# Expert weights read in runs of 16 KB, two or four adjacent rows a partition

## The chip, the cores and the metric

One core of one Trainium2 chip runs the whole program. The metric is the device time of one execution in microseconds, the median of several runs; lower is better.

## What is computed

One decoder layer on 256 tokens of width 1024, in float32: a recurrent branch and an attention branch are mixed, and then comes a mixture of 32 experts, of which each token takes 4. The experts are what this case is about:

```python
N_EXPERTS = 32; TOP_K = 4; D_MODEL = 1024; D_EXPERT = 1024   # 256 tokens

def expert_block(args):
    xb, e = args
    gu = xb @ w_gu[e] + b_gu[e]                      # w_gu[e]: 1024 x 2048
    x_glu = jnp.minimum(gu[:, :D_EXPERT], SWIGLU_LIMIT)
    x_lin = jnp.clip(gu[:, D_EXPERT:], -SWIGLU_LIMIT, SWIGLU_LIMIT)
    act = x_glu * jax.nn.sigmoid(SWIGLU_ALPHA * x_glu) * (x_lin + 1.0)
    return act @ w_down[e] + b_down[e]               # w_down[e]: 1024 x 1024
```

Every expert's weights are read whole: 8 MB of `w_gu` and 4 MB of `w_down` each, 384 MB in all.

## The kernel before

Each engine has one program, written out by hand, and semaphores join them. SyncE (SP) issues nearly all DMAs, in one queue, in the order of its code; a wait in SP's code holds everything behind it.

First come 20 blocks of 2 MB of the dense matrices (`w_in`, `w_proj_rnn`, `w_proj_attn`, `w_out`), which land in two buffers `land` and are split by ScalarE (`w_hi`) and GpSimd (`w_lo`) for TensorE; SP loads block u when `lo_ready` says that block u - 2 is done with (L260). Between these blocks, SP already loads what it can of experts 0 and 1 into places that earlier tiles have left: parts of gate and up weights ("gu") of expert 1 at u = 11, 12, 14, 15 and 16, parts of the down weights ("dn") of expert 0 at u = 13 and 18, the rest behind the last block (L294 to L312). The semaphore `filled` counts finished halves of the dense products (40 in all), `lg_filled` the router's logits.

Then come the experts. gu has two sets of eight 1 MB buffers (`gu[par][k]`, one for each step k of 128 rows of the contraction), dn one set of four buffers of 1 MB (`dn[j]`, two k-steps each; the last is filled by two DMAs). SP reloads a gu buffer when `gu_used` says that TensorE has finished with it two experts before, a dn buffer when `dn_used` says so one expert before. In the loop up to expert 15 (`TURN` = 8 pairs) the queue holds gu of expert e + 1 ahead of dn of expert e; from then on it is gu(e), dn(e), gu(e + 1).

TensorE's part of an expert (`expert`, L617 to L673): bias rows, 32 gate and up matmuls (L635) with the 64 tokens of the expert (`xg`) as weights, transposes of the gates (L643), the gather of the next expert's tokens (L587), some matmuls that only keep the clock up (L394), four transposes of the activation (L654), 16 down matmuls (L663), and four that add the weighted rows to the sums (L670). A float32 matmul shows as two records. VectorE's part, between the gate matmuls and the transposes: clamp the gate half (L1171) and the up half (L1172) out of PSUM, join them (L1174), multiply by ScalarE's sigmoid (L1178), take the next expert's tokens out of PSUM into `xg` (L1145), and copy the transposed activation (L1182).

Ahead of the experts, L1084 (VectorE, tokens 0 to 127) and L848 (ScalarE, the others) write the normalised tokens `hn`; the first gather (L600) reads them as weights, 128 channels at a time, and L1152 scales them by the norm's vector `V_GFFN`. So the contraction's channels are cut into eight runs of 128 adjacent ones, like the rows of `w_gu`.

Of the kernel before, what the change touches and what calls it, by code (L numbers as in the profile page):

```python
# [52 lines left out]
V_GMIX, V_CONVW, V_CONVB, V_BX, V_BA, V_AP, V_GFFN, N_VEC = 0, 1, 5, 6, 7, 8, 9, 10  # L53


def program(nc, x, vecs, rope, w_in, lru_wx, lru_wa, w_proj_rnn, w_proj_attn, w_out,
# [7 lines left out]
    with ctx:  # L64
# [43 lines left out]
        x1T, hn = at("x1T", 24, [P, KT, T]), at("hn", 168, [P, TT, D])  # L108
# [6 lines left out]
        gu = [[at(f"gu{par}_{k}", 96 * par + 8 * k, [P, 2 * D]) for k in range(KT)] for par in range(2)]  # L115
        dn = [at(f"dn{j}", 64 + 8 * j, [P, 2, D]) for j in range(4)]
# [53 lines left out]

        x_landed = [sem(f"x_landed{t}") for t in range(TT)]
# [4 lines left out]
        gu_landed = [[sem(f"gu_landed{p}_{k}") for k in range(KT)] for p in range(2)]  # L176
        dn_landed = [sem(f"dn_landed{j}") for j in range(5)]
# [56 lines left out]
        def _(sp):  # L234
# [8 lines left out]
            def load_gu(row, par, wait, ks=range(KT)):  # L243
                for k in ks:
                    wait(k)
                    sp.dma_start(gu[par][k][:, :], w_gu_rows[ds(row + k * P, P), :]).then_inc(gu_landed[par][k], 16)  # L246

            def load_dn(row, wait, js=range(4)):
                for j in js:
                    wait(j)  # L250
                    src = w_dn_rows[ds(row + j * 2 * P, 2 * P), :].rearrange("(k p) n -> p k n", p=P)
                    if j < 3:
                        sp.dma_start(dn[j][:, :, :], src).then_inc(dn_landed[j], 16)  # L253
                    else:
                        for c in range(2):
                            sp.dma_start(dn[j][:, c, :], src[:, c, :]).then_inc(dn_landed[j + c], 16)  # L256

            for u, src in enumerate(blocks):
# [35 lines left out]
                if u == 11:  # L294
                    load_gu(D, 1, lambda k: sp.wait_ge(b96_landed, 48), [3])
                if u == 12:
                    load_gu(D, 1, lambda k: sp.wait_ge(hglo_ready, 1), [5])
                if u == 13:
                    load_dn(0, lambda j: sp.wait_ge(hg_ready, 1), [3, 2])
                if u in (14, 15):  # L300
                    load_gu(D, 1, lambda k: sp.wait_ge(s_filled, H), [u - 14])
                if u == 16:
                    load_gu(D, 1, lambda k: sp.wait_ge(filled, 28), [2])
                if u == 18:
                    load_dn(0, lambda j: sp.wait_ge(filled, 32), [1])
            load_dn(0, lambda j: sp.wait_ge(filled, 36), [0])
            load_gu(D, 1, lambda k: sp.wait_ge(filled, 36), [4])
            load_gu(D, 1, lambda k: sp.wait_ge(mix_ready, 4), [6, 7])
            load_gu(0, 0, lambda k: sp.wait_ge(lo_ready, 76 if k < 2 else 80), range(0, 3))
            load_gu(0, 0, lambda k: sp.wait_ge(filled, 39), [4, 6])  # L310
            load_gu(0, 0, lambda k: sp.wait_ge(filled, 40), [5, 7])
            load_gu(0, 0, lambda k: sp.wait_ge(lg_filled, 1), [3])  # L312

            def load_pair(E, row):
                load_gu(row, 0, lambda k: sp.wait_ge(gu_used, KT * E + (k + 1 - 2 * KT)))
                load_dn(row, lambda j: sp.wait_ge(dn_used, 4 * E + (j + 1 - 4)))
                load_gu(row + D, 1, lambda k: sp.wait_ge(gu_used, KT * E + (k + 1 - KT)))
# [70 lines left out]
        def _(pe):  # L388
# [228 lines left out]
            def expert(E, X, par, meanwhile=None, first=False):  # L617
# [622 lines left out]
```

## Time and profile before

| | us |
|---|---|
| median of 3 runs | 1256.97 (1255.77 to 1258.02) |
| span of the profiled execution | 1254.1 |
| TensorE busy | 1174.0 (94%) |
| VectorE, ScalarE, GpSimd busy | 341.2, 219.5, 221.3 |
| DMA queue of SP, share of the 16 engines | 89.5%, 449.07 MB |

The span is that of one profiled execution, from first to last instruction; the profile does not give that execution a time of its own, and the median lies 2.9 us above the span. The page cuts the span into 40 slices and gives for each the busy share of an engine in tenths (9 is 90% or more), the clock that TensorE was granted, and what the DMA engines moved:

```profile
## 2 busy tenths in 40 slices
PE   8969789999999999999999999999999999999996
...
PEclk9989999999999999999999999999999999999998
DMA  9434446679899999999999999999999999999994
GB/s 255 164 134 143 142 165 245 229 260 383 343 417 416 417 418 418 418 418 418 418 418 418 418 413 418 418 418 418 418 418 417 418 418 418 418 418 418 418 417 197
```

A slice is 31.4 us. The first nine or so are the dense part, the rest the experts.

### The profile page before, as it was taken

How to read it: one execution, taken by the hardware profiler on the slowest of the kernel's cores; microseconds unless marked ns; L12 is line 12 of the kernel's file. 1: busy time of each engine (PE TensorE's matmuls, PEld its weight loads, DVE VectorE, ACT ScalarE, POOL GpSimd, SP SyncE). 2: the span in 40 equal slices, each digit the busy share in tenths (PEclk: the TensorE clock that was granted, in tenths of full speed). 3: DMA queues.
4: the chain of work that ended last, by engine and by line, in shares of the span. 5: the costliest groups of instructions: out<-in, count | busy, mean ns of one | idle time of the engine just before them, and what ended most of it. 6: DMA issues, size and time to landing. Idle time of an engine off the chain costs nothing.

```text
span 1254.1 us, 18900 instructions
## 1 busy us (share of the span) xinstructions
PE 1174.0 (94%) x7653; PEld 604.0 (48%) x7653; DVE 341.2 (27%) x595; ACT 219.5 (17%) x361; POOL 221.3 (18%) x99
## 2 busy tenths in 40 slices
PE   8969789999999999999999999999999999999996
PEld 8859789999333333333333333333333333333332
DVE  5972685332311111221111111111211111111112
ACT  5436635545100000000000000000000000000001
POOL 6838966784000000000000000000000000000000
PEclk9989999999999999999999999999999999999998
DMA  9434446679899999999999999999999999999994
GB/s 255 164 134 143 142 165 245 229 260 383 343 417 416 417 418 418 418 418 418 418 418 418 418 413 418 418 418 418 418 418 417 418 418 418 418 418 418 418 417 197
DMA packets 98784, 450.03 MB, mean 359 GB/s; under 512 B 10721, under 2 KB 12833, under 8 KB 65825
## 3 DMA queue, kind: packets, MB, share of 16 engines
q1 hardware_dynamic: 98608, 449.07, 89.5%
q8 instruction: 22, 0.36, 0.1%
q0 software_dynamic: 144, 0.52, 0.1%
q14 instruction: 10, 0.07, 0.0%
HBM read 448.00 MB, written 1.05 MB: 358 GB/s over the span
## 4 chain that ended last, share of the span: by engine, by line
PE 60%; DMA 14%; issue 7%; SPq 7%; POOL 7%; ACT 2%; DVE 2%; POOLq 0%; DVEq 0%
PE ps L635 25%; PE ps L663 13%; DMA gu<-in_w_gu 10%; POOL w_lo L368 6%; DMA dn<-in_w_down 4%; PE ps L670 3%; SPq L246 3%; PE ps L587 3%; PE ps L394 2%; PE ps L421 2%; PE ps L418 2%; PE ps L417 2%; SPq L253 2%; SPq L256 2%; DVE actT L1182 1%
## 5 line engine op out<-in xcount | busy, mean ns | idle before, releaser
L635 PE MATMUL ps<-gu,xg 128*64 128x512 f32 x2048 | 448.9, 593 | 7.2 <-DMA gu<-in_w_gu 7.2
L635 PEld LDWEIGHTS ps<-gu,xg 128*64 128x64 f32 x2048 | 142.0, 137 | 296.0 <-issue 263.8
L663 PE MATMUL ps<-dn,actT 128*64 128x512 f32 x1024 | 228.1, 596 | 10.3 <-DVE actT L1182 6.0
L368 POOL TENSOR_TENSOR w_lo<-land,w_hi 128x1024 fp32r<-128x1024 f32 x80 | 216.1, 2729 | 76.1 <-ACT w_hi L715 76.0
L1171 DVE TENSOR_SCALAR g<-ps 128x512 f32<-128x512 f32 x32 | 22.1, 692 | 746.4 <-PE ps L635 746.4
L663 PEld LDWEIGHTS ps<-dn,actT 128*64 128x64 f32 x1024 | 72.0, 137 | 154.0 <-issue 137.5
L863 ACT ACTIVATE wT<-ps 128x256 f32<-128x256 f32 x32 | 12.3, 384 | 539.3 <-PE ps L643 539.3
L417 PE MATMUL ps<-x_hi,w_hi 128*128 128x256 f32 x384 | 95.8, 287 | 4.1 <-ACTq L753 2.9
L418 PE MATMUL ps<-x_lo,w_hi 128*128 128x256 f32 x384 | 94.9, 284 | 0.0
L715 ACT ACTIVATE w_hi<-land 128x1024 fp32r<-128x1024 f32 x80 | 80.1, 1052 | 55.1 <-PE ps L421 39.4
L670 PE MATMUL ps<-y_sb,wT 64*128 64x512 f32 x256 | 63.6, 615 | 22.2 <-ACT y_sb L869 22.2
L869 ACT ACTIVATE y_sb<-ps 128x512 f32<-128x512 f32 x32 | 19.1, 597 | 329.4 <-PE ps L663 329.4
L417 PEld LDWEIGHTS ps<-x_hi,w_hi 128*128 128x128 f32 x384 | 74.1, 193 | 4.5 <-issue 4.5
L418 PEld LDWEIGHTS ps<-x_lo,w_hi 128*128 128x128 f32 x384 | 74.2, 193 | 0.1
L394 PE MATMUL ps<-ones 128*128 128x512 bf16 x254 | 66.8, 386 | 0.0
L421 PE MATMUL ps<-x_hi,w_lo 128*128 128x256 f32 x384 | 55.2, 287 | 5.2 <-POOL w_lo L368 5.2
L670 PEld LDWEIGHTS ps<-y_sb,wT 64*128 64x128 f32 x256 | 22.0, 186 | 65.4 <-ACT y_sb L869 50.4
L421 PEld LDWEIGHTS ps<-x_hi,w_lo 128*128 128x128 f32 x384 | 50.2, 194 | 6.6 <-POOL w_lo L368 6.4
L587 PE MATMUL ps<-sel,part 128*128 128x64 bf16 x1536 | 50.0, 193 | 0.0
L587 PEld LDWEIGHTS ps<-sel,part 128*128 128x128 bf16 x1536 | 49.2, 98 | 0.4
L394 PEld LDWEIGHTS ps<-ones 128*128 128x128 bf16 x254 | 23.0, 99 | 15.7 <-issue 0.8
L1182 DVE COPY actT<-ps 128x512 f32<-128x512 f32 x32 | 22.1, 692 | 7.7 <-PE ps L654 3.2
(246 smaller groups left out, 929.0 us busy)
## 6 DMA issues: line engine op xcount, KB each, us to landing
gu<-in_w_gu SPq DMA_DIRECT2D x256, 1024.0 KB, 19.3
dn<-in_w_down SPq DMA_DIRECT2D x96, 1024.0 KB, 19.7
dn<-in_w_down SPq DMA_DIRECT2D x64, 512.0 KB, 17.9
land<-in_w_in SPq DMA_DIRECT2D x13, 2048.0 KB, 8.0
land<-in_w_proj_rnn SPq DMA_DIRECT2D x2, 2048.0 KB, 8.9
land<-in_w_proj_attn SPq DMA_DIRECT2D x2, 2048.0 KB, 8.9
land<-in_w_out SPq DMA_DIRECT2D x2, 2048.0 KB, 7.8
land<-in_w_in SPq DMA_DIRECT2D x2, 1024.0 KB, 8.8
```

The lines of the kernel that those rows point to most:

```text
L246: sp.dma_start(gu[par][k][:, :], w_gu_rows[ds(row + k * P, P), :]).then_inc(gu_landed[par][k], 16)
L368: pool.tensor_tensor(w_lo[:, q % PIECES], land[q // PIECES][:, :, (q % PIECES) * P:(q % PIECES + 1) * P], w_hi[:, q % PIECES].bitcast(f32) ...
L394: mm(ps[:, bank, :], ones[:, :], ones[:, :].unsqueeze(1).to_broadcast([P, 4, P]), start=True, stop=True)
L417: mm(to, w_hi[:, b, k, :], src_hi[:, k, :], start=k == 0, stop=False)
L418: mm(to, w_hi[:, b, k, :], src_lo[:, k, :], start=False, stop=False)
L421: last = mm(to, w_lo[:, b, k, :], src_hi[:, k, :], start=False, stop=k == KT - 1)
L587: last = mm(ps[:, 6, k * SLOTS:(k + 1) * SLOTS], part[q][:, t, k * P:(k + 1) * P], sel[buf][:, t, :], start=n == 0, stop=n == 3 * TT - 1)
L635: last = mm(ps[64 * h:64 * h + 64, 4 + c, :], xg[:, k * SLOTS:(k + 1) * SLOTS], gu[par][k][:, c * D + h * HALF:c * D + (h + 1) * HALF], st ...
L663: last = mm(ps[64 * h:64 * h + 64, 6, :], actT[:, k % 4, (k // 4) * SLOTS:(k // 4 + 1) * SLOTS], dn[k // 2][:, k % 2, h * HALF:(h + 1) * H ...
L670: mm(ps[:, 2 * t + h, :], wT[64 * h:64 * h + 64, t * P:(t + 1) * P], y_sb[64 * h:64 * h + 64, :], start=False, stop=False)
L715: A(w_hi[:, q % PIECES], land[u % LAND][:, :, (q % PIECES) * P:(q % PIECES + 1) * P], ACT.Copy).then_inc(hi_ready, 1)
L1182: V.tensor_copy(actT[:, :, :], ps[:, 7, :].rearrange("p (j s) -> p j s", j=4)).then_inc(actT_ready, 1)
```

## The change

- The rows of `w_gu` are cut another way. A buffer is now 2 MB, and partition p gets two adjacent rows of 8 KB, rows 8p + 2m and 8p + 2m + 1 for buffer m, in one run of 16 KB. k-step k then contracts the channels 8p + k. One DMA fills one buffer: four an expert, not eight.
- `w_down` likewise: a buffer holds half of the rows, partition p four adjacent rows of 4 KB (16 KB). Two DMAs of 2 MB an expert, not five.
- The channels of the tokens are reordered to match: L1084 and L848 read `x_sb` with a step of 8 elements and write `hn` contiguously, and the norm's vector is there a second time in that order (`V_GROW`).
- The columns of the activation are reordered to match `w_down`: L1171 and L1172 read PSUM with a step of 4 elements and write contiguously.
- `gu_used`, `dn_used` and the landing semaphores count 4 and 2 an expert. The early loads sit at other places in the queue, and `x1T` moves from 24 KB to 184 KB, so that the last gu buffers of expert 0 no longer wait for the logits.

```diff
-        x1T, hn = at("x1T", 24, [P, KT, T]), at("hn", 168, [P, TT, D])
+        x1T, hn = at("x1T", 184, [P, KT, T]), at("hn", 168, [P, TT, D])
...
-        gu = [[at(f"gu{par}_{k}", 96 * par + 8 * k, [P, 2 * D]) for k in range(KT)] for par in range(2)]
-        dn = [at(f"dn{j}", 64 + 8 * j, [P, 2, D]) for j in range(4)]
+        gu = [[at(f"gu{par}_{m}", 96 * par + 16 * m, [P, GU_RUN, 2 * D]) for m in range(4)] for par in range(2)]
+        dn = [at(f"dn{h}", 64 + 16 * h, [P, DN_RUN, D]) for h in range(2)]
...
+        hn_rows = hn[:, :, :].rearrange("q t (k p) -> q t k p", k=KT)
+        x_rows = x_sb[:, :, :].rearrange("q t (p k) -> q t k p", k=KT)
+
+        def by_rows(t):
+            return t.rearrange("q (j p) -> q j p", j=DN_RUN)
+
+        def by_columns(t):
+            return t.rearrange("q (p j) -> q j p", j=DN_RUN)
...
-            def load_gu(row, par, wait, ks=range(KT)):
-                for k in ks:
-                    wait(k)
-                    sp.dma_start(gu[par][k][:, :], w_gu_rows[ds(row + k * P, P), :]).then_inc(gu_landed[par][k], 16)
-
-            def load_dn(row, wait, js=range(4)):
-                for j in js:
-                    wait(j)
-                    src = w_dn_rows[ds(row + j * 2 * P, 2 * P), :].rearrange("(k p) n -> p k n", p=P)
-                    if j < 3:
-                        sp.dma_start(dn[j][:, :, :], src).then_inc(dn_landed[j], 16)
-                    else:
-                        for c in range(2):
-                            sp.dma_start(dn[j][:, c, :], src[:, c, :]).then_inc(dn_landed[j + c], 16)
+            def load_gu(row, par, wait, ms=range(4)):
+
+                src = w_gu_rows[ds(row, D), :].rearrange("(p k) n -> p k n", p=P)
+                for m in ms:
+                    wait(m)
+                    sp.dma_start(gu[par][m][:, :, :], src[:, GU_RUN * m:GU_RUN * m + GU_RUN, :]).then_inc(
+                        gu_landed[par][m], 16)
+
+            def load_dn(row, wait, hs=range(2)):
+
+                for h in hs:
+                    wait(h)
+                    src = w_dn_rows[ds(row + h * HALF, HALF), :].rearrange("(p j) n -> p j n", p=P)
+                    sp.dma_start(dn[h][:, :, :], src).then_inc(dn_landed[h], 16)
...
-                if u == 11:
-                    load_gu(D, 1, lambda k: sp.wait_ge(b96_landed, 48), [3])
-                if u == 12:
-                    load_gu(D, 1, lambda k: sp.wait_ge(hglo_ready, 1), [5])
                 if u == 13:
-                    load_dn(0, lambda j: sp.wait_ge(hg_ready, 1), [3, 2])
-                if u in (14, 15):
-                    load_gu(D, 1, lambda k: sp.wait_ge(s_filled, H), [u - 14])
+                    load_dn(0, lambda h: sp.wait_ge(hg_ready, 1), [1])
+                if u == 15:
+                    load_gu(D, 1, lambda m: sp.wait_ge(s_filled, H), [0])
                 if u == 16:
-                    load_gu(D, 1, lambda k: sp.wait_ge(filled, 28), [2])
-                if u == 18:
-                    load_dn(0, lambda j: sp.wait_ge(filled, 32), [1])
-            load_dn(0, lambda j: sp.wait_ge(filled, 36), [0])
-            load_gu(D, 1, lambda k: sp.wait_ge(filled, 36), [4])
-            load_gu(D, 1, lambda k: sp.wait_ge(mix_ready, 4), [6, 7])
-            load_gu(0, 0, lambda k: sp.wait_ge(lo_ready, 76 if k < 2 else 80), range(0, 3))
-            load_gu(0, 0, lambda k: sp.wait_ge(filled, 39), [4, 6])
-            load_gu(0, 0, lambda k: sp.wait_ge(filled, 40), [5, 7])
-            load_gu(0, 0, lambda k: sp.wait_ge(lg_filled, 1), [3])
+                    load_gu(D, 1, lambda m: sp.wait_ge(filled, 28), [1])
+            load_dn(0, lambda h: sp.wait_ge(filled, 36), [0])
+            load_gu(D, 1, lambda m: sp.wait_ge(filled, 36), [2])
+            load_gu(D, 1, lambda m: sp.wait_ge(mix_ready, 4), [3])
+            load_gu(0, 0, lambda m: sp.wait_ge(lo_ready, 76 + 4 * m), [0, 1])
+            load_gu(0, 0, lambda m: sp.wait_ge(filled, 40), [2, 3])
...
-                load_gu(i * (2 * D), 0, lambda k: sp.wait_ge(gu_used, KT * (2 * i) + (k + 1 - 2 * KT)))
-                load_dn(i * (2 * D) - D, lambda j: sp.wait_ge(dn_used, 8 * i + (j + 1 - 8)))
-                load_gu(i * (2 * D) + D, 1, lambda k: sp.wait_ge(gu_used, KT * (2 * i) + (k + 1 - KT)))
-                load_dn(i * (2 * D), lambda j: sp.wait_ge(dn_used, 8 * i + (j + 1 - 4)))
-            load_dn((2 * TURN - 1) * D, lambda j: sp.wait_ge(dn_used, 8 * TURN + (j + 1 - 8)))
+                load_gu(i * (2 * D), 0, lambda m: sp.wait_ge(gu_used, 4 * (2 * i) + (m + 1 - 8)))
+                load_dn(i * (2 * D) - D, lambda h: sp.wait_ge(dn_used, 4 * i + (h + 1 - 4)))
+                load_gu(i * (2 * D) + D, 1, lambda m: sp.wait_ge(gu_used, 4 * (2 * i) + (m + 1 - 4)))
+                load_dn(i * (2 * D), lambda h: sp.wait_ge(dn_used, 4 * i + (h + 1 - 2)))
+            load_dn((2 * TURN - 1) * D, lambda h: sp.wait_ge(dn_used, 4 * TURN + (h + 1 - 4)))
...
-                for k in range(KT):
-                    pe.wait_ge(gu_landed[par][k], 8 * E + 16)
-                    if first and k == 4:
+                for m in range(4):
+                    pe.wait_ge(gu_landed[par][m], 8 * E + 16)
+                    if first and m == 2:
                         pe.wait_ge(xg_ready, 1)
-                    for c in range(2):
-                        for h in range(2):
-                            last = mm(ps[64 * h:64 * h + 64, 4 + c, :], xg[:, k * SLOTS:(k + 1) * SLOTS],
-                                      gu[par][k][:, c * D + h * HALF:c * D + (h + 1) * HALF],
-                                      start=False, stop=k == KT - 1)
+                    for r in range(GU_RUN):
+                        k = GU_RUN * m + r
+                        for c in range(2):
+                            for h in range(2):
+                                last = mm(ps[64 * h:64 * h + 64, 4 + c, :], xg[:, k * SLOTS:(k + 1) * SLOTS],
+                                          gu[par][m][:, r, c * D + h * HALF:c * D + (h + 1) * HALF],
+                                          start=False, stop=k == KT - 1)
                     last.then_inc(gu_used, 1)
...
-                for k in range(KT):
-                    if k % 2 == 0 or k == KT - 1:
-                        pe.wait_ge(dn_landed[(k + 1) // 2], 16 * E + 16 * (par + 1))
-                    for h in range(2):
-                        last = mm(ps[64 * h:64 * h + 64, 6, :], actT[:, k % 4, (k // 4) * SLOTS:(k // 4 + 1) * SLOTS],
-                                  dn[k // 2][:, k % 2, h * HALF:(h + 1) * HALF], start=k == 0, stop=k == KT - 1)
-                    if k % 2 == 1:
-                        last.then_inc(dn_used, 1)
+                for half in range(2):
+                    pe.wait_ge(dn_landed[half], 16 * E + 16 * (par + 1))
+                    for j in range(DN_RUN):
+                        for h in range(2):
+                            last = mm(ps[64 * h:64 * h + 64, 6, :], actT[:, j, half * SLOTS:(half + 1) * SLOTS],
+                                      dn[half][:, j, h * HALF:(h + 1) * HALF],
+                                      start=half == 0 and j == 0, stop=half == 1 and j == DN_RUN - 1)
+                    last.then_inc(dn_used, 1)
...
-            A(hn[:, 1, :], x_sb[:, 1, :], ACT.Copy, scale=rstd2[:, 1:2]).then_inc(hn_ready, 1)
+            A(hn_rows[:, 1], x_rows[:, 1], ACT.Copy, scale=rstd2[:, 1:2]).then_inc(hn_ready, 1)
...
-            V.tensor_scalar(hn[:, 0, :], x_sb[:, 0, :], rstd2[:, 0:1], None, ALU.mult).then_inc(hn_ready, 1)
+            V.tensor_scalar(hn_rows[:, 0], x_rows[:, 0], rstd2[:, 0:1], None, ALU.mult).then_inc(hn_ready, 1)
...
-                dve.wait_ge(gu_used, KT * E + KT * (par + 1))
-                V.tensor_scalar(g1[:, :], ps[:, 4, :], LIMIT, None, ALU.min).then_inc(glu_ready, 1)
-                V.tensor_scalar(l1[:, :], ps[:, 5, :], LIMIT, -LIMIT, ALU.min, ALU.max).then_inc(gu_read, 1)
+                dve.wait_ge(gu_used, 4 * E + 4 * (par + 1))
+                V.tensor_scalar(by_rows(g1[:, :]), by_columns(ps[:, 4, :]), LIMIT, None, ALU.min).then_inc(glu_ready, 1)
+                V.tensor_scalar(by_rows(l1[:, :]), by_columns(ps[:, 5, :]), LIMIT, -LIMIT, ALU.min, ALU.max).then_inc(gu_read, 1)
```

## Rows read from the trace of the kernel before

**Rows 1.** Windows: range, us, busy PE, PEld, DVE, ACT, POOL, clock, DMA share, GB/s.

```profile
318.00:1235.00 917.00, 877.56 (x5402) 325.86 (x5400) 158.43 (x354) 52.75 (x99) 0.70 (x1) 1.00 1.02 417
```

**Rows 2.** Chain of waits inside one expert: start us, us, what (x records).

```profile
403.11 13.73 PE ps L635 x64
...
416.84 0.37 PE ps L643 x2
...
418.61 1.08 PE ps L394 x5
...
421.20 7.11 PE ps L663 x32
...
431.52 8.58 PE ps L635 x39
```

**Rows 3.** The first clamp's line: duration ns min/median/max, first and last start.

```profile
L1171 DVE TENSOR_SCALAR g<-ps x32: 691/692/693, 328.9 to 1228.7; 128x512 f32<-128x512 f32 x32
```

**Rows 4.** Chain of waits at other experts, same columns as rows 2.

```profile
315.06 13.73 PE ps L635 x64
...
374.69 13.74 PE ps L635 x64
...
648.54 3.67 PE ps L663 x16
...
749.08 13.74 PE ps L635 x64
...
976.40 13.73 PE ps L635 x64
```

**Rows 5.** Waits: engine, line, releaser: us in total, times, longest.

```profile
PEld ps L635 <- DMA gu<-in_w_gu: 26.5, 27, 1.5
...
PEld ps L663 <- DMA dn<-in_w_down: 15.1, 18, 1.5
```

**Rows 6.** Packets and bytes of the whole span, from the page.

```profile
DMA packets 98784, 450.03 MB, mean 359 GB/s; under 512 B 10721, under 2 KB 12833, under 8 KB 65825
```

**Rows 7.** Windows, columns as rows 1; in the first two only gu moves, then only dn.

```profile
354.00:370.00 16.00, 15.39 (x120) 6.30 (x118) 4.90 (x11) 1.38 (x3) 0.00 (x0) 1.00 1.01 421
...
1147.00:1163.00 16.00, 15.31 (x74) 4.86 (x70) 0.00 (x0) 0.60 (x1) 0.00 (x0) 1.00 1.01 420
...
374.00:380.00 6.00, 6.00 (x32) 2.09 (x32) 0.00 (x0) 0.00 (x0) 0.00 (x0) 1.00 1.03 412
...
494.00:500.00 6.00, 6.00 (x30) 1.97 (x28) 0.00 (x0) 0.00 (x0) 0.00 (x0) 1.00 1.02 408
```

**Rows 8.** Windows around the first expert, columns as rows 1.

```profile
278.00:296.00 18.00, 17.98 (x148) 17.59 (x147) 3.45 (x5) 8.83 (x13) 15.01 (x7) 1.00 1.00 407
296.00:300.00 4.00, 4.00 (x36) 4.00 (x35) 0.69 (x1) 2.67 (x10) 1.78 (x7) 1.00 0.56 193
...
313.00:319.00 6.00, 6.00 (x38) 3.05 (x39) 5.15 (x8) 2.76 (x3) 0.00 (x0) 1.00 0.23 66
```

**Rows 9.** VectorE ahead of the experts: two lines, and where L1089 starts (start us, us).

```profile
L1084 DVE TENSOR_SCALAR hn<-x_sb,stat x1: 754/754/754, 306.4 to 306.4; 128x1024 f32<-128x1024 f32 x1
...
L1162 DVE TENSOR_TENSOR hn<-hn,part x2: 1217/1218/1219, 314.9 to 316.0; 128x1024 f32<-128x1024 f32 x2
...
307.55 0.41 DVE L1089 SCALAR_TENSOR_TENSOR lg<-ps,stat,rbb 128x32 f32<-128x32 f32 x2 [0.42 <-PE ps L547]
```

**Rows 10.** VectorE between gate and down matmuls of one expert: start us, us, operation.

```profile
416.89 0.69 DVE L1171 TENSOR_SCALAR g<-ps 128x512 f32<-128x512 f32 x1 [23.30 <-PE ps L635]
...
418.94 0.69 DVE L1178 TENSOR_TENSOR act_s<-l,act_s 128x512 f32<-128x512 f32 x1
```

**Rows 11.** Two lines that read PSUM contiguously: 256 and 512 elements a partition.

```profile
L1152 DVE TENSOR_TENSOR xg<-ps,vec x2: 425/425/425, 312.8 to 314.6; 128x256 f32<-128x256 f32 x2
...
L1145 DVE TENSOR_TENSOR xg<-ps,vec x32: 681/683/685, 331.5 to 1231.4; 128x512 f32<-128x512 f32 x32
```

More of the change, by code:

```diff
@@ L50 @@
 LOW, HIGH = -3.0e38, 3.0e38
-V_GMIX, V_CONVW, V_CONVB, V_BX, V_BA, V_AP, V_GFFN, N_VEC = 0, 1, 5, 6, 7, 8, 9, 10
+V_GMIX, V_CONVW, V_CONVB, V_BX, V_BA, V_AP, V_GFFN, V_GROW, N_VEC = 0, 1, 5, 6, 7, 8, 9, 10, 11
+GU_RUN = 2
+DN_RUN = 4
 def program(nc, x, vecs, rope, w_in, lru_wx, lru_wa, w_proj_rnn, w_proj_attn, w_out,
@@ L175, in program @@
         hi_ready, lo_ready, filled, evicted = sem("hi_ready"), sem("lo_ready"), sem("filled"), sem("evicted")
-        gu_landed = [[sem(f"gu_landed{p}_{k}") for k in range(KT)] for p in range(2)]
-        dn_landed = [sem(f"dn_landed{j}") for j in range(5)]
+        gu_landed = [[sem(f"gu_landed{p}_{m}") for m in range(4)] for p in range(2)]
+        dn_landed = [sem(f"dn_landed{h}") for h in range(2)]
         (vec_landed, rope_landed, wx_landed, wa_landed, b96_landed, rw_landed, rbb_landed,
@@ L314, in load_pair @@
+            load_gu(D, 1, lambda m: sp.wait_ge(mix_ready, 4), [3])
+            load_gu(0, 0, lambda m: sp.wait_ge(lo_ready, 76 + 4 * m), [0, 1])
+            load_gu(0, 0, lambda m: sp.wait_ge(filled, 40), [2, 3])
             def load_pair(E, row):
-                load_gu(row, 0, lambda k: sp.wait_ge(gu_used, KT * E + (k + 1 - 2 * KT)))
-                load_dn(row, lambda j: sp.wait_ge(dn_used, 4 * E + (j + 1 - 4)))
-                load_gu(row + D, 1, lambda k: sp.wait_ge(gu_used, KT * E + (k + 1 - KT)))
@@ L318, in load_pair @@
-                load_dn(row + D, lambda j: sp.wait_ge(dn_used, 4 * E + (j + 1)))
+                load_gu(row, 0, lambda m: sp.wait_ge(gu_used, 4 * E + (m + 1 - 8)))
+                load_dn(row, lambda h: sp.wait_ge(dn_used, 2 * E + (h + 1 - 2)))
+                load_gu(row + D, 1, lambda m: sp.wait_ge(gu_used, 4 * E + (m + 1 - 4)))
+                load_dn(row + D, lambda h: sp.wait_ge(dn_used, 2 * E + (h + 1)))
             with sp.Fori(1, TURN, 1) as i:
-                load_gu(i * (2 * D), 0, lambda k: sp.wait_ge(gu_used, KT * (2 * i) + (k + 1 - 2 * KT)))
@@ L867, in expert @@
                     meanwhile()
-                act.wait_ge(dn_used, 4 * E + 4 * (par + 1))
+                act.wait_ge(dn_used, 2 * E + 2 * (par + 1))
                 A(y_sb[:, :], ps[:, 6, :], ACT.Copy).then_inc(y_ready, 1)
@@ L1146, in take_tokens @@
                                 ps[:, 6, :].rearrange("p (k s) -> p k s", k=KT),
-                                vec[:, V_GFFN, :].unsqueeze(2).to_broadcast([P, KT, SLOTS]), ALU.mult).then_inc(
+                                vec[:, V_GROW, :].unsqueeze(2).to_broadcast([P, KT, SLOTS]), ALU.mult).then_inc(
                     xg_ready, 1)
@@ L1153, in _ @@
                                 ps[:, 6 + half, 0:256].rearrange("p (k s) -> p k s", k=4),
-                                vec[:, V_GFFN, 4 * half:4 * half + 4].unsqueeze(2).to_broadcast([P, 4, SLOTS]),
+                                vec[:, V_GROW, 4 * half:4 * half + 4].unsqueeze(2).to_broadcast([P, 4, SLOTS]),
                                 ALU.mult).then_inc((xg_half, xg_ready)[half], 1)
@@ L1215 @@
     rows = [a["norm_mix_g"][0], *a["conv_w"][0], a["conv_b"][0], a["lru_bx"][0], a["lru_ba"][0], a["lru_a_param"][0],
-            a["norm_ffn_g"][0]]
+            a["norm_ffn_g"][0], a["norm_ffn_g"][0].reshape(P, KT).T.reshape(D)]
     vecs = np.ascontiguousarray(np.stack(rows).reshape(N_VEC, KT, P).transpose(2, 0, 1).reshape(P, N_VEC * KT))
```

## Prediction

> **What bounds the kernel now.** I read the windows by stage first. From 318 to 1235 us, through nearly all of the 32 experts, the DMA engines are full (share 1.02) and move 417 GB/s, while TensorE is busy for 877.56 of 917 us at a full granted clock [rows 1]. An expert has 8 MB of gate and up weights and 4 MB down, 12.58 million bytes, which is 30.17 us at 417 GB/s. So there are two limits close together, and the next view, the chain of waits inside one expert, gives the other one. From the start of one expert's first matmul to the next (403.11 to 431.52) it is 28.41 us, and every link is TensorE, VectorE or ScalarE, no transfer [rows 2]. TensorE alone would take 28.41 us an expert, the transfers 30.17.
>
> That the kernel isn't simply as slow as its transfers comes from a lead: 16 to 20 MB are in the buffers when the experts begin. The first clamp (L1171) starts at 328.9 and the last at 1228.7, 899.8 us for 31 steps [rows 3]. 31 steps of 28.41 are 880.7. The first two steps hold work of their own (315.06 to 374.69, where two steps of 28.41 end at 371.9) [rows 4], 2.8 us together. The rest, **16.3 us, is all that the weights still cost**. The waits that end on gu and dn transfers say the same in kind [rows 5], but they overlap matmuls still in the pipe, so I go by the starts. In two places the steps slip: expert 15 starts at 749.08 where 374.69 plus 13 steps is 744.0 (5.1 us; the break is in the down matmuls of expert 11, at 648.54), and from expert 23, which started on time at 976.40, to the last clamp another 11.3 (976.40 + 8 x 28.41 + 13.73 = 1217.4, not 1228.7) [rows 2 to 4].
>
> **The transfers.** The packets become 16 KB; now they are 8 KB for gu and 4 KB for dn (a packet is one row of the matrix; 98784 - 65825 = 32959 packets are of 8 KB or more [rows 6], gu has 32768 rows). In windows in which only one kind moves, gu runs at 420 to 421 GB/s and dn at 408 to 412 (six windows like the first two, seven like the last two) [rows 7]. With 421 and 409.5, one of 16 engines takes 8192 x 16 / 421 = 311.3 ns for 8 KB and 160.0 ns for 4 KB. Two 4 KB packets cost 8.7 ns more than one of 8 KB: that is the price of a packet. 16 KB in one is then 613.9 ns, 427 GB/s. An expert takes 29.47 us instead of 30.17. No row has a 16 KB weight packet. One bound is the rate of 8 KB packets (nothing more to gain, 421 GB/s, 29.89 us), the other no packet price at all (303 ns for 8 KB, 432 GB/s, 29.1 us). I take 29.47, since the step from 4 to 8 KB is in these rows.
>
> The trace's price of a packet is 8.7 ns. The Trainium skill, "DMA: Bandwidth & Descriptors", section "Why small descriptors are slow (HBM only)", has about 3 cycles a packet (some 3.5 ns at its 850 MHz). By that alone an expert would gain 0.3 us, not 0.7, and the result would be close to the second rival below. The difference of the two rates here speaks for the larger price.
>
> **What the faster transfers are worth.** TensorE stays at 28.41, so the transfers fall behind by 1.06 us an expert instead of 1.76. Now the lead broke first after 11.75 experts, 20.7 us behind. After expert 16 the order of the queue changes (TURN: dn ahead of the next gu); then it broke at expert 23, 23.75 x 1.76 - 5.1 = 36.7 us behind. After the change it is 16 x 1.06 = 17.0 at the turn and 31 x 1.06 = 32.9 at the last expert. Coarser pieces eat some lead: a gu buffer comes free after two k-steps instead of one (13.73 / 8 = 1.72 us later) and a piece of 2 MB lands 2.5 us after one of 1 MB would have; the dn halves are alike (7.11 / 4 = 1.78 us). That is 4.2 us of lead, not of time: 21.2 against 20.7, 37.1 against 36.7. So nearly all of the 16.3 us goes, and I leave 1.0 us of stall (0 to 5, the rate of the 16 KB packet decides: 0.1 us an expert is 3 us by the end). What is late next is TensorE, which caps the gain at 16.3 however fast the DMAs are.
>
> **The head of the queue.** Loads that were spread over u = 11 to 18 move to 13, 15 and 16. None makes a wait of its own: SP waits there for the landing buffers anyway, and a 2 MB piece (5 us) fits in the 12 to 15 us between two of them. After the wait on `filled` 36 there are 14 MB to load instead of 12. Now the queue holds 407 GB/s in 278 to 296, has a hole in 296 to 300 (193 GB/s), and is all but idle in 313 to 319 (66 GB/s), full buffers waiting for expert 0 [rows 8]. The added 2 MB (5 us) fit in these holes, and the last piece lands near 316, where expert 0 reads it at 315.06 + 6 x 1.72 = 325. The wait for `lg_filled` falls away. Cost 0. If the holes were not there it would be up to 5 us.
>
> **The moved x1T, the vector column, the fewer semaphores.** Same instructions, same shapes, other addresses: 0.
>
> **The reordered norm.** L1084 and L848 read `x_sb` with a step of 8 elements. L1084 takes 754 ns for 1024 elements where L1162, at about one element a cycle, takes 1.22 us [rows 9]. If the step costs the fast mode it ends 0.46 us later, at 307.6, and L1089 (307.55 [rows 9]) hardly moves; if each element costs twice that, 1.1 us. L1089 starts the VectorE chain to the first gather, so this is on the path, once. I take 0.6. L848's output isn't wanted before that gather.
>
> **The clamps, 64 times.** L1171 and L1172 now read PSUM with a step of 4 elements (16 bytes) and write contiguously. They are on the path: from the last gate matmul (416.84) TensorE waits for VectorE's four operations of 0.68 to 0.69 us one behind another (416.89 to 419.63), then transposes, and has only clock-keeping matmuls to fill with [rows 2, 10]. Queued behind the clamps on VectorE are L1174, L1178, the next tokens and L1182. So each ns on a clamp is two an expert, 64 in all. No row reads PSUM with a step. Lower bound 0: for 256 more elements L1145 pays 683 - 425 = 258 ns over L1152 [rows 11], 1.0 ns an element, so VectorE is at one element a cycle already, and the memory gives more than that: TensorE writes 512 columns of it in 1.08 / 5 = 0.216 us [rows 2]. A gain is excluded, as nothing is taken off the operation. Upper bound: each element costs twice, 512 x 1.0 = 0.51 us a clamp, 32.6 us in all. I take 0, because the rate that TensorE gets leaves room for a second access per element.
>
> Speaking against the change: the Trainium skill, "PSUM — Partial Sum Buffer", section "Specifications (TRN2)", gives lines of 8 bytes and says that any non-contiguous pattern "slows matmuls significantly". It has no figure for VectorE. With one element a line TensorE's write rate above would halve to 1.2 elements a ns, still above VectorE's 1.0, so rule and row allow 0 together; if the rule held for VectorE too, the time would be the first rival's.
>
> **Sum.** -16.3 + 1.0 + 0.6 + 0 = -14.7. The span goes from 1254.1 to 1239.4; the median of the runs is 2.9 above the span, so 1256.97 becomes **1242.3 us**. Its own range is 1240.5 (no stall) to 1247 (5 us of it).
>
> **Rivals.**
> 1. The step in PSUM costs VectorE a second cycle. Place: L1171 and L1172. An expert becomes 28.41 + 1.02 = 29.43 us for TensorE, no transfer is late any more (29.47), and 1256.97 - 16.3 + 0.6 + 32.6 gives 1274. It decides for slower from 14.7 / 64 = 0.23 us a clamp. For it: both clamps are unhidden. Against: TensorE's rate into the same memory. A price of 0.05 to 0.2 us would leave 1246 to 1255.
> 2. 16 KB packets run no faster than 8 KB ones, and only dn gains. 29.89 us an expert, 1.48 behind: 23.7 + 4.2 - 20.7 = 7.2 us of stall by the turn, then 45.9 - 7.2 + 4.2 - 36.7 = 6.2. 1256.97 - 16.3 + 13.4 + 0.6 = 1254.7. For it: 421 is near what this queue ever reaches in the windows. Against: the step from 409.5 to 421.
> 3. The change doesn't do what it says: a partition's 16 KB lie 64 KB from the next partition's in gu, and the total rate stays at 417. Then the coarser pieces cost their 4.2 us: 1256.97 + 4.2 + 0.6 = 1261.8. No row supports a slower pitch.
>
> **How the numbers follow.** Forecast 0.57; small price on the clamps 0.06; rival 1 0.22; rival 2 0.09; rival 3 0.06. About 0.2% (2.5 us) is what a measurement can tell from no change. Faster: 0.57 + 0.06 and a third of rival 2, less a little for forecasts that miss by more, 0.65. Same: the rest of rival 2 and the edges, 0.08. Slower: rivals 1 and 3, 0.27. The range, 1240 to 1262, leaves out rival 1 and little else.
>
> **What would show it.** L1171 and L1172 at 0.69 and 0.68 us (0.9 or more: rival 1). GB/s of the saturated windows 425 to 429 while the queue is full, and below it late in the run, when it waits for buffers (421: rival 2). Steps of 28.41 us from expert 2 to 31, with the last L1171 near 1214. Waits on gu and dn transfers under 3 us. L1084 between 1.2 and 2.3 us. Steps above 28.5 with no late transfer would prove the forecast wrong.

## The result and the profile after

The changed kernel takes 1243.14 us (median, 1242.14 to 1243.84); the kernel before, timed beside it, 1257.12. The ratio is 0.9893, 95% interval 0.9881 to 0.9905: faster by 1.1%, 14.0 us. A second comparison (e9 below) has 1241.75 against 1256.17, ratio 0.9879 (0.9862 to 0.9896). The forecast was 1242.3.

The page of the changed kernel, parts of it: span, busy tenths of TensorE and of the DMA engines in 40 slices, GB/s, and the packets.

```profile
span 1241.5 us, 18076 instructions
...
PE   7969879999999999999999999999999999999996
...
DMA  8434426659899999999999989999999999999994
GB/s 248 175 135 143 145 88 252 238 210 422 366 409 428 428 428 429 427 431 428 428 428 429 429 358 429 431 429 427 429 429 430 427 429 429 429 427 430 429 428 168
DMA packets 54238, 450.01 MB, mean 362 GB/s; under 512 B 7136, under 2 KB 9248, under 8 KB 29472
```

From the 13th slice to the last but one it is 427 to 431 GB/s, but for one of 358, where before it was 416 to 418, but for one of 413. There are 54238 packets instead of 98784 [rows 6]. The windows by stage (range, us, busy PE, PEld, DVE, ACT, POOL, clock, DMA share, GB/s) put the low slice in place:

```profile
400.00:600.00 200.00, 193.65 (x1196) 72.53 (x1192) 34.29 (x77) 11.19 (x21) 0.00 (x0) 1.00 1.01 428
720.00:740.00 20.00, 19.79 (x136) 7.78 (x134) 4.90 (x11) 1.00 (x2) 0.00 (x0) 1.00 0.84 343
740.00:760.00 20.00, 19.31 (x113) 6.66 (x108) 0.81 (x2) 1.05 (x3) 0.00 (x0) 1.00 0.96 407
800.00:1000.00 200.00, 193.64 (x1196) 72.78 (x1195) 34.30 (x77) 11.19 (x21) 0.00 (x0) 1.00 1.01 428
```

428 GB/s against the 417 of [rows 1], TensorE as busy as it was. In 720 to 760 the queue runs dry for a while: at 428 GB/s it would have moved the same bytes in 5.0 us less (4.0 in the first 20 us, 1.0 in the next). The forecast did not have that. The first clamp, whose starts give the length of each expert's step ([rows 3] before):

```profile
L1178 DVE TENSOR_SCALAR g<-ps x32: 690/691/693, 330.1 to 1215.7; 128x512 f32<-128x512 f32 x32
```

From 330.1 to 1215.7 it is 885.6 us for 31 steps, where before it was 899.8. The steps one by one, as differences of these starts: 30.57 and 29.07, then 28.42 or 28.43 for each expert up to the last two, 29.29 and 29.35. Before, ten steps were late, nine of them 30.02 to 30.15 and one 29.39 (the steps to experts 13 to 15 and 25 to 31), the others 28.41. By the steps the gain is 14.2 us, by the medians 14.0. (The spans of the two profiled executions are only 12.6 us apart: in this one expert 0 came 1.2 us later, as e9 shows below.) The waits of PEld that end on weights are 4.3 us on gu and 0.5 us on dn, against the 26.5 and 15.1 of [rows 5] (columns: us in total, times, longest):

```profile
PEld ps L642 <- DMA gu<-in_w_gu: 4.3, 5, 1.6
...
PE ps L642 <- DMA gu<-in_w_gu: 1.4, 2, 0.7
...
PEld ps L670 <- DMA dn<-in_w_down: 0.5, 1, 0.5
```

### The profile page after: what moved, and what is told of

Same layout as the page of the kernel before. It is cut to its first block, busy times and chain, and to the rows that moved or that the text cites. A ratio compares the mean times of both kernels' runs of the same rounds, so it can differ in the third digit from the quotient of the medians.

```text
span 1241.5 us, 18076 instructions
## 1 busy us (share of the span) xinstructions
PE 1166.6 (94%) x7653; PEld 604.1 (49%) x7653; DVE 341.7 (28%) x595; ACT 220.6 (18%) x361; POOL 222.3 (18%) x99
## 2 busy tenths in 40 slices
DMA packets 54238, 450.01 MB, mean 362 GB/s; under 512 B 7136, under 2 KB 9248, under 8 KB 29472
## 4 chain that ended last, share of the span: by engine, by line
PE 76%; issue 7%; POOL 5%; DVE 4%; DMA 4%; ACT 3%; SPq 0%; POOLq 0%; DVEq 0%
PE ps L642 33%; PE ps L670 18%; POOL w_lo L373 5%; PE ps L677 5%; PE ps L592 3%; DMA gu<-in_w_gu 3%; PE ps L399 3%; PE ps L426 2%; PE ps L422 2%; PE ps L423 2%; DVE actT L1189 2%; PE ps L661 2%; ACT y_sb L876 1%; PE ps L632 1%; PE ps L650 1%
## 5 line engine op out<-in xcount | busy, mean ns | idle before, releaser
L677 PE MATMUL ps<-y_sb,wT 64*128 64x512 f32 x256 | 63.6, 615 | 22.2 <-ACT y_sb L876 22.2
L399 PEld LDWEIGHTS ps<-ones 128*128 128x128 bf16 x254 | 22.7, 98 | 15.2
```

Of the source, the lines that this page charges most:

```text
L399: mm(ps[:, bank, :], ones[:, :], ones[:, :].unsqueeze(1).to_broadcast([P, 4, P]), start=True, stop=True)
L677: mm(ps[:, 2 * t + h, :], wT[64 * h:64 * h + 64, t * P:(t + 1) * P], y_sb[64 * h:64 * h + 64, :], start=False, stop=False)
```

## The experiments

All of them start from the changed kernel. "Step" is the time from one expert's first clamp to the next one's.

**e1, the short runs.** The same 2 MB buffers, transfers, semaphores and queue, but rows 128 apart in a partition again.

```diff
-                src = w_gu_rows[ds(row, D), :].rearrange("(p k) n -> p k n", p=P)
+                src = w_gu_rows[ds(row, D), :].rearrange("(k p) n -> p k n", p=P)
-                    src = w_dn_rows[ds(row + h * HALF, HALF), :].rearrange("(p j) n -> p j n", p=P)
+                    src = w_dn_rows[ds(row + h * HALF, HALF), :].rearrange("(j p) n -> p j n", p=P)
-            V.tensor_scalar(hn_rows[:, 0], x_rows[:, 0], rstd2[:, 0:1], None, ALU.mult).then_inc(hn_ready, 1)
+            V.tensor_scalar(hn[:, 0, :], x_sb[:, 0, :], rstd2[:, 0:1], None, ALU.mult).then_inc(hn_ready, 1)
```

(L855 and both clamps likewise go back to the old form, and `V_GROW` to `V_GFFN`.)

> The changed kernel with its buffers, its 2 MB transfers, its queue and its semaphores, but with rows 128 apart in a partition as before: packets of 8 KB and 4 KB again, and no reordering of channels or columns. Theory (the packet's length is what counts): saturated windows at 417 GB/s, TensorE late by 1.76 us an expert, stalls of 16 to 20 us on gu and dn, median 1257 to 1262. Rival (fewer and larger transfers, or the new places in the queue, brought the gain): 425 GB/s or more, or at least a median under 1248.

Measured: 1262.42 us, ratio 1.0053 (1.0036 to 1.007), slower than before. Its window by stage and its first clamp:

```profile
400.00:600.00 200.00, 192.82 (x1192) 72.35 (x1192) 34.29 (x77) 11.55 (x22) 0.00 (x0) 1.00 1.02 417
```

```profile
L1178 DVE TENSOR_SCALAR g<-ps x32: 690/692/693, 328.7 to 1234.8; 128x512 f32<-128x512 f32 x32
```

417 GB/s, as before the change. So for the rate the length of the run is what counts, not the size of a transfer (0.5 and 1 MB before, 2 MB here). What is left of the change without its long runs costs 6.4 us over the 1256.03 of that comparison. The late steps hold 6.2 of them, 22.35 us against 16.15, so this is in the main the price of coarse pieces. The first late step comes after nine instead of twelve on time, which costs 4.1 us by expert 15, and the steps behind the turn cost 2.1 us more. A step on the transfers' pace is 30.12 us, as it was. Stalls and median came out just above what I had written (20 us, 1262).

**e2 and e3, one matrix at a time.** e2 keeps the long runs of gu and takes the dn lines (and the clamps) of e1; e3 keeps dn and takes the gu lines and the old token order.

> Only gu in 16 KB runs; dn in 4 KB packets, columns of the activation in the old order (clamps contiguous). By the price of a packet as the two traces have it (12.45 ns saved for each pair of 8 KB joined), an expert takes about 0.40 us less than 30.17: 29.8. The lead then runs out: 1.4 us an expert behind, stalls of 8 to 13 us, median 1250 to 1254.

> Only dn in 16 KB runs; gu in 8 KB packets, tokens in the old order. Four 4 KB packets joined save 38 ns, 0.6 us an expert: 29.6, so 1.2 us behind, stalls of 4 to 9 us, median 1246 to 1250, below e2. If packets had no price of their own and only the row pitch counted, e2 and e3 would not add up to the whole.

Measured: e2 1254.43 us, 0.9987 (0.9977 to 0.9996); e3 1249.28 us, 0.9948 (0.9932 to 0.9965). The same window of e2, then of e3:

```profile
400.00:600.00 200.00, 192.97 (x1194) 72.58 (x1194) 34.28 (x77) 11.80 (x22) 0.00 (x0) 1.00 1.01 422
```

```profile
400.00:600.00 200.00, 193.67 (x1196) 72.92 (x1198) 34.28 (x77) 11.21 (x21) 0.00 (x0) 1.00 1.01 424
```

The late steps, where an expert goes at the pace of its transfers, are 29.82 in e2 and 29.67 in e3. Both expectations had the order right and the price too high: I had taken 12.45 and 38 ns from the durations of single packets in the traces, and these overlap (share of the DMA engines 1.01 to 1.02). The late steps cost 14.2 us in e2 and 10.1 in e3, each about 1 us more than the 8 to 13 and 4 to 9 that I had written, and e2 at 1254.43 is just outside its range. The two savings, 0.30 and 0.45 us, add up: 29.37 us an expert, and the 428 GB/s of the changed kernel are 29.40.

**e4, the step on the other side of the clamps.**

```diff
-                V.tensor_scalar(by_rows(g1[:, :]), by_columns(ps[:, 4, :]), LIMIT, None, ALU.min).then_inc(glu_ready, 1)
+                V.tensor_scalar(g1[:, :].rearrange("q (j p) -> q p j", j=DN_RUN), ps[:, 4, :].rearrange("q (p j) -> q p j", j=DN_RUN), LIMIT, None, ALU.min).then_inc(glu_ready, 1)
```

(The clamp of `l1` likewise.)

> The changed kernel with the step of the two clamps on the side of the write into SBUF (128 elements, 512 bytes) and PSUM read contiguously. Theory (both clamps are on the path, each ns 64 times): if the write costs x more a clamp, the median is 1243.1 + 64 x, less the 1.8 us of stall that slower experts no longer have. With x = 0.35 us (1.7 ns an element instead of 1.0) 1264; with x = 0, 1243. Rival (clamps are hidden by other work): no change whatever x is.

Measured: 1260.58 us, ratio 1.0035 (1.0022 to 1.0048). The first clamp:

```profile
L1178 DVE TENSOR_SCALAR g<-ps x32: 1070/1072/1076, 329.1 to 1233.1; 128x512 f32<-128x512 f32 x32
```

1.07 us instead of 0.69, so x is 0.38 by duration. Each step of an expert is 29.12 instead of 28.42, 0.35 a clamp: the second clamp already starts 0.9 us after the first. 29 steps of 0.70 less the 1.8 us of late steps that are gone make 18.5, and the clamps' starts show 18.4. (The first two steps stay at 30.56 and 29.06, so it is 58 clamps and not the 64 of my formula, which with x = 0.38 gives 1265.6.) So the clamps are on the path, and a change like this one with the step on the write side would have been slower than the kernel before.

**e11, a long step in PSUM.** The other way round: `g1` is written with `"q (p j) -> q p j"` (contiguously) and `ps[:, 4, :]` read with `"q (j p) -> q p j"`, a step of 512 bytes.

> The changed kernel with the clamps reading PSUM with a step of 128 elements (512 bytes) instead of 4, writing contiguously. The columns then stand in an order that w_down's rows don't have, so the output is not the reference's. Theory (VectorE reads PSUM at one element a cycle whatever the step): 0.69 and 0.68 us a clamp, steps of 28.42, 1243. Rival (16 bytes is just inside what is free): 0.9 to 1.2 us a clamp, as the write into SBUF with a step of 512 bytes had (1.07), and 1256 or more.

Measured: 1241.82 us, 0.9881 (0.9863 to 0.99).

```profile
L1178 DVE TENSOR_SCALAR g<-ps x32: 690/691/693, 328.7 to 1214.3; 128x512 f32<-128x512 f32 x32
```

As with a step of 16 bytes, and as with none. (Its output has the columns in another order than `w_down` wants; it serves for the time alone.)

**e5 and e10, the turn of the queue.**

```diff
-            load_dn((2 * TURN - 1) * D, lambda h: sp.wait_ge(dn_used, 4 * TURN + (h + 1 - 4)))
+            E0, row0 = 2 * TURN, 2 * TURN * D
+            load_gu(row0, 0, lambda m: sp.wait_ge(gu_used, 4 * E0 + (m + 1 - 8)), [0, 1])
+            load_dn(row0 - D, lambda h: sp.wait_ge(dn_used, 2 * E0 + (h + 1 - 4)))
+            load_gu(row0, 0, lambda m: sp.wait_ge(gu_used, 4 * E0 + (m + 1 - 8)), [2, 3])
+            load_dn(row0, lambda h: sp.wait_ge(dn_used, 2 * E0 + (h + 1 - 2)))
+            load_gu(row0 + D, 1, lambda m: sp.wait_ge(gu_used, 4 * E0 + (m + 1 - 4)))
+            load_dn(row0 + D, lambda h: sp.wait_ge(dn_used, 2 * E0 + (h + 1)))
```

(and the second loop of SP starts at TURN + 1)

> The changed kernel with another order at the turn of the queue (expert 16): half of gu(16) goes ahead of dn(15), the other half behind it, so that SP has work in the queue while it waits for dn_used. Now the queue runs dry there (windows 735 to 740: 111 GB/s), some 5 us of transfers lost. Theory (lead is what the end lacks): with 5 us more lead the two late steps at the end (29.29 and 29.35, 1.8 us) become 28.42, median 1241.3. Rival (the end is late for another reason): those two steps stay, 1243.1.

> The changed kernel itself, on the same chip as the next run, so that the two can be compared: 1243, ratio 0.989. Its first gate matmul has come at 316.30 where others of its kind had 315.4: if that was one execution's chance in the first load, it comes near 315 here.

> The kernel of e5 once more beside the changed one. Theory (the hole at the turn costs the last two steps): 1.2 to 2.2 us below the run before it. Rival (the two medians of before differ only by chance): within 0.6 us.

Measured: e5 1240.86 us, 0.9875 (0.9858 to 0.9891); then, on one chip, e9 1241.75, 0.9879 (0.9862 to 0.9896), and e10 1240.32, 0.9866 (0.9848 to 0.9883). Two windows of e10:

```profile
720.00:740.00 20.00, 19.79 (x136) 7.82 (x134) 4.90 (x11) 1.00 (x2) 0.00 (x0) 1.00 1.01 428
760.00:780.00 20.00, 19.09 (x92) 6.58 (x92) 2.71 (x8) 0.60 (x1) 0.00 (x0) 1.00 0.86 347
```

720 to 740 is full now, but 760 to 780 has 347 GB/s. The hole moved by an expert and is 3.8 us of transfers instead of 5.0 to 5.2 (e9 has 321 and 423 GB/s in 720 to 760), so the 5 us more lead that e5 was to bring were not had. Of the late steps at the end 0.86 us stayed in e10 (29.28) and 1.2 us in all in e5 (28.61 at the turn, 29.38 at the end), against 1.64 in e9 (28.77, 29.71). By the steps the new order brings 0.8 us; the medians of e10 and e9, taken on one chip, are 1.4 apart, within what the theory had, and the slowest run of e10 (1241.08) lies below the fastest of e9 (1241.54). These are four runs of each, and the intervals of their ratios overlap: some gain is likely, its size isn't settled. e10 was the fastest complete kernel of the study.

What the hole hangs on shows in the DMAs that SP issues in the changed kernel (start us, us, what):

```profile
742.21 0.34 SPq L269 DMA_DIRECT2D dn<-in_w_down  x1
742.90 2.11 SPq L261 DMA_DIRECT2D gu<-in_w_gu  x4
```

The last half of dn(15) goes out when TensorE has ended the down matmuls of expert 14, and gu(16) stands behind it, though its buffers had been free since about 731, when expert 14's gate and up matmuls ended. In e10 the same happens one expert later: gu(17) goes out at 769.55, behind dn(16).

e9 also settles a point of the traces. The changed kernel's first load landed late in the profiled execution shown above (ScalarE's first split of it starts at 11.27 us, in e9 at 9.23), and its first gate matmul comes at 316.13; in e9, the same kernel, it comes at 314.73 and the last clamp at 1214.1:

```profile
L1178 DVE TENSOR_SCALAR g<-ps x32: 690/692/693, 328.7 to 1214.1; 128x512 f32<-128x512 f32 x32
```

**e6, no transfer can be late.** From expert 1 on, only half of the columns of `w_down` are loaded, which leaves out part of the down product.

(`cols` is HALF, and D for the two loads of expert 0.)

```diff
-                    sp.dma_start(dn[h][:, :, :], src).then_inc(dn_landed[h], 16)
+                    sp.dma_start(dn[h][:, :, 0:cols], src[:, :, 0:cols]).then_inc(dn_landed[h], 16)
```

> The changed kernel with half the columns of every dn piece left out from expert 1 on (2 KB packets; the output is not the reference's for these columns). 10.5 MB an expert, about 25 us: no transfer can be late. Theory (TensorE's own 28.42 caps the gain): all steps 28.42, only the last 1.8 us go, 1241 to 1242. Rival (full DMA engines slow the engines or the matmuls in other ways): steps under 28.3 and a median under 1240.

Measured: 1240.3 us, 0.9871 (0.9855 to 0.9888).

```profile
L1178 DVE TENSOR_SCALAR g<-ps x32: 691/692/692, 329.2 to 1212.9; 128x512 f32<-128x512 f32 x32
```

Every step from the third on is 28.41 or 28.42, and the last clamp starts at 1212.9. The median is 0.7 us under what I had written. This is the floor that the chain of TensorE and VectorE sets: all faster transfers together could still bring 1.4 to 2.8 us (against 1241.75 and 1243.14).

**e7, runs of 32 KB for gu.** `GU_RUN = 4`, two buffers of 4 MB a set, the waits and counts for two pieces an expert.

```diff
-GU_RUN = 2
+GU_RUN = 4
-        gu = [[at(f"gu{par}_{m}", 96 * par + 16 * m, [P, GU_RUN, 2 * D]) for m in range(4)] for par in range(2)]
+        gu = [[at(f"gu{par}_{m}", 96 * par + 32 * m, [P, GU_RUN, 2 * D]) for m in range(2)] for par in range(2)]
```

> gu in runs of 32 KB, two 4 MB transfers an expert; dn unchanged. Price of a packet about 9 to 12 ns, so an expert takes 0.15 to 0.2 us less (29.15), saturated windows near 431 GB/s. But a buffer comes free 3.4 us later and lands 4.9 us later: 8.3 us less lead. Theory (coarseness costs lead, not time): stalls of 3 to 7 us instead of 1.8, median 1244 to 1249. Rival (longer is better): under 1243.

Measured: 1244.27 us, 0.9906 (0.989 to 0.9923).

```profile
400.00:600.00 200.00, 192.96 (x1194) 72.74 (x1194) 34.26 (x77) 11.80 (x22) 0.00 (x0) 1.00 1.00 430
```

430 GB/s and late steps of 29.22 us, 0.07 above what I had written. But the late steps are five (28.87 and four of 29.22 to 29.23) and cost 3.7 us instead of 1.6 to 1.8: faster transfers, no faster kernel.

**e8, x1T at its old place.**

```diff
-        x1T, hn = at("x1T", 184, [P, KT, T]), at("hn", 168, [P, TT, D])
+        x1T, hn = at("x1T", 24, [P, KT, T]), at("hn", 168, [P, TT, D])
-            load_gu(0, 0, lambda m: sp.wait_ge(lo_ready, 76 + 4 * m), [0, 1])
-            load_gu(0, 0, lambda m: sp.wait_ge(filled, 40), [2, 3])
+            load_gu(0, 0, lambda m: sp.wait_ge(lo_ready, 76), [0])
+            load_gu(0, 0, lambda m: sp.wait_ge(filled, 40), [2, 3])
+            load_gu(0, 0, lambda m: sp.wait_ge(lg_filled, 1), [1])
```

> The changed kernel with x1T at its old place, so that the second gu piece of expert 0 waits for the router's logits and is issued last, near 309 us. It lands near 320 where TensorE wants it at 319.7: expert 0 is 0 to 3 us late, and the queue starts its full stretch as late, median 1243 to 1246. If the head of the queue has no slack at all, more.

Measured: 1244.55 us, 0.9911 (0.9894 to 0.9927). The chain at expert 0 (start us, us, what) goes through the piece that waited:

```profile
307.11 12.66 DMA gu<-in_w_gu
319.82 10.52 PE ps L643 x48
```

Issued at 307.11, landed at 319.8, and TensorE, idle for 1.75 us, takes it up at once. From the start of L1092 (the norm, 305.95) to the first clamp it is 24.4 us, against 22.2 to 22.8 in the others.

**The price of a packet.** The paces of the late steps fall on one line. A packet is one run: a row, or the two or four rows that lie together. Packets an engine and expert (gu rows plus dn rows, over 16) and the pace:

| | packets | pace, us | GB/s in 400 to 600 |
|---|---|---|---|
| before, e1 | 128 | 30.12 | 417 |
| e2, gu 16 KB | 96 | 29.82 | 422 |
| e3, dn 16 KB | 80 | 29.67 | 424 |
| changed | 48 | 29.35 (last step) | 428 |
| e7, gu 32 KB | 32 | 29.22 | 430 |

0.30 us for 32 packets, 0.45 for 48 and 0.90 for 96 are 9.4 ns each time. For the changed kernel the line gives 29.37. Its own 29.35 is a single step of one execution and no steady pace (the last step is 29.71 in e9, 29.38 in e8, 29.42 in e11), so the line rests on the other four rows; its 428 GB/s, 29.40 us, agree with it.

Carried on to no packets at all, the line is at 28.92 us, 435 GB/s. That is an estimate, beyond what any run has. It would still be above TensorE's 28.42: by it not even a longer run would let the transfers keep up with TensorE, and only lead, or fewer bytes as in e6, hides the difference.

## Why the prediction was right, point by point

- **The two limits and the cap.** TensorE's 28.41 us an expert was right and did not move (28.42), and the gain ended there, as written. e6 shows that nothing but the late steps was to be had.
- **The price of a packet.** Predicted 8.7 ns and 427 GB/s from the windows in which one kind moves [rows 7]; measured 9.4 ns and 428. Right in mechanism (e1), near in size. The Trainium skill's 3 cycles a packet ("DMA: Bandwidth & Descriptors", section "Why small descriptors are slow (HBM only)"), an estimated 3.5 ns, are not what this queue shows: 9.4 ns over runs of 4 to 32 KB. Rival 2, which stood beside that figure, is out: 16 KB runs are faster than 8 KB ones, and 32 KB ones faster yet.
- **Lead.** Predicted cost of the coarser pieces: 4.2 us of lead. Before, it broke after 12 steps of 28.41 against a pace of 30.12, 12 x 1.71 = 20.5 us; in e1 after 10 x 1.71 less the 0.6 of the first late step (29.04) = 16.5. That is 4.0. Rival 3 was this mechanism at an unchanged rate, forecast at 1261.8; e1 had 1262.4. That the two are so close is in part luck: the rival counted the lead once, 4.2 us, and 0.6 for a reordered norm that e1 doesn't have, over 1256.97, while e1 lost 6.4 us over 1256.03. The 2.1 us that it lost behind the turn the rival left out; there e1 has a hole too, 352 GB/s of 417 in 740 to 760.
- **The stall that stays.** Predicted 1.0 us (0 to 5), measured 1.8 in the profiled execution and 1.64 in e9. This is the term that was mis-sized, and that it is near is luck, as two errors in its sum cancel. The transfers fall behind by 0.95 us an expert (29.37 against 28.42), not 1.06; with that the sum has 15.2 + 4.2 = 19.4 us at the turn against the 20.7 at which the lead breaks, and 29.5 + 4.2 = 33.7 at the end against 36.7, so nothing would be late. And the sum left out the hole at the turn. With its 5.0 us the end comes to 38.7, 2.0 us late, and with the 3.8 us of e10 to 37.5, 0.8 us late; measured are 1.6 to 1.8, and 0.86. These are estimates, but they fit. Half of the 1.0 us I had put at the turn (expert 16), and nothing was late there.
- **Why there is a hole.** I had counted lead as if it could only be used up. At the turn the queue stands still when it has landed all that was issued and waits for `dn_used`. How long this lasts depends on how far the buffers are ahead: in e6, where the transfers are far ahead, 720 to 740 has 11 GB/s. But e1 has a hole as well, though its steps were late up to expert 15, and the kernel before, with 1 MB pieces and late steps, has none (410 GB/s in 735 to 750, what it has where dn moves). So lead in excess isn't all of it, and the size of the pieces seems to have a share; no run takes the two apart.
- **The head of the queue.** Predicted 0. The holes of [rows 8] did take the added 2 MB:

```profile
278.00:296.00 18.00, 17.98 (x148) 17.59 (x147) 4.20 (x6) 8.15 (x10) 15.01 (x8) 1.00 1.03 426
296.00:300.00 4.00, 4.00 (x36) 4.00 (x36) 0.69 (x1) 2.34 (x10) 3.29 (x7) 1.00 0.97 414
...
316.00:320.00 4.00, 4.00 (x24) 1.31 (x22) 4.00 (x5) 2.53 (x3) 0.00 (x0) 1.00 0.24 98
```

  (Columns as above; 426 and 414 GB/s where there were 407 and 193, and the idle stretch in 316 to 320.) But I wrote the moved `x1T` off at 0 as an address only, and named the wait that falls away beside it without a price. e8 shows that the 2 MB piece would have been 1.6 to 2.2 us late there (24.4 us from the norm to the first clamp against 22.2 to 22.8). Before, the waiting piece was of 1 MB, and TensorE took it fourth.
- **The norm.** Predicted 0.6 us. The two lines now:

```profile
L1091 DVE TENSOR_SCALAR hn<-x_sb,stat x1: 1153/1153/1153, 307.9 to 307.9; 128x1024 f32<-128x1024 f32 x1
...
L855 ACT ACTIVATE hn<-x_sb,stat x1: 2162/2162/2162, 307.9 to 307.9; 128x1024 f32<-128x1024 f32 x1
```

  The next step of the chain:

```profile
309.07 0.41 DVE L1096 SCALAR_TENSOR_TENSOR lg<-ps,stat,rbb 128x32 f32<-128x32 f32 x2
```

  VectorE's norm is 1.15 us: 0.40 more than before and still under my lower case (1.22). That it costs nothing shows at that next step, L1089 before and L1096 now. Before, it started 1.17 us after the norm, and VectorE had been idle for 0.42 us, waiting for TensorE [rows 9]. Now it starts at 309.07, again 1.17 us after the norm (307.90), and without a wait. So the longer norm fills a wait that was there; I took the middle of my two cases, where the lower one, worked out as hardly anything, was right. ScalarE's went from 1.15 to 2.16 us, which I had not priced. It is hidden, as said: it ends at 310.06, and the gather starts at 311.96. From the start of the norm to the first clamp it is 22.5 us before, 22.2 and 22.5 in the kernels without the reordering (e3, e1), and 22.2 to 22.8 with it. I can't tell that from 0.
- **The clamps.** Predicted 0, with most of the chances resting on it, and 0 it was. The second of them:

```profile
L1179 DVE TENSOR_SCALAR l<-ps x32: 679/680/682, 330.7 to 1216.3; 128x512 f32<-128x512 f32 x32
```

  680 ns as before, and 691 for the first. The reason given (TensorE's rate into PSUM leaves room) was an argument, not shown; e11 shows the fact for a step of 512 bytes too. The Trainium skill's sentence on PSUM ("PSUM — Partial Sum Buffer", section "Specifications (TRN2)") speaks of matmuls, and for VectorE's reads no run shows any price. Rival 1's place and weight were real: e4 pays 17.4 us in the median for 0.35 us a clamp (18.5 when each kernel is set against the one before in its own comparison). Its decision point, 0.23 us, fits: e4 is past it and slower than before.
- **The sum.** -14.7 predicted; -14.0 and -14.4 in the two comparisons. Terms: late steps 16.3 before, 1.6 to 1.8 after; the norm's 0.6 not there. The two misses, 0.8 us too little stall and 0.6 us too much norm, cancel; that 1242.3 comes to lie between the two medians is partly luck. Two figures of the prediction don't follow from its own terms, and nothing hangs on them: no stall gives 1241.3 and 5 us of it 1246.3, not 1240.5 and 1247, and twice L1162's time would end the norm 1.3 us after L1089's start, not 1.1.

The chain of waits at the end of the changed kernel shows what is left: expert 29 on time, and at expert 31, the last, TensorE waits for a gu piece that had been issued 41 us before it landed.

```profile
1143.30 13.73 PE ps L642 x64
...
1161.39 7.11 PE ps L670 x32
...
1170.96 41.02 DMA gu<-in_w_gu
1212.02 3.65 PE ps L642 x16
1215.67 0.37 PE ps L650 x2
```

Open: the same kernel has 1243.14 in one comparison and 1241.75 in another, with the kernel before 0.95 us apart; in the profiled executions ScalarE takes up the first load of the dense part 2.0 us later in one of them, and the first gate matmul comes 1.4 us later. No run here takes that apart.

## What to carry to other kernels

Where a queue is saturated, look at its rate in windows in which only one size of run moves; two sizes give the price of a packet, and what a longer run would bring can then be added up. Ask next what the other limit is (here 28.41 against 30.17 us an expert) and what the coarser pieces take from the lead, since e1 and e7 show that coarseness alone costs as much as a moderate gain in rate brings. Look too at where the order of the queue changes: a load that waits for its buffer holds back the ones behind it whose buffers are free. And where data must be reordered to match, put the step where reading is free: the same permutation cost nothing on the read of PSUM and made the kernel slower than before on the write into SBUF.

## What the runs showed of the hardware

- A packet of a weight load costs 9.4 ns beside its bytes, from 4 to 32 KB (e1, e2, e3, e7).
- VectorE reads PSUM, float32, 512 elements, in 691 or 692 ns with a step of 4 bytes, 16 bytes or 512 bytes. Writing SBUF with a step of 512 bytes takes 1072 ns, 0.74 ns an element more, of which 0.35 of 0.38 us come onto the path.
- Reading SBUF with a step of 32 bytes, 1024 elements, VectorE needs 1153 ns instead of 754, ScalarE 2162 instead of 1149.
- Runs of a partition that lie 64 KB apart in HBM (gu) or side by side (dn) made no difference that these runs could tell: both fall on the line of 9.4 ns.
